# The last attention step of a diffusion-transformer layer: output projection in two banks, h in halves, top-k candidates filled in place

## Chip, cores and metric

The kernel runs on one core of a Trainium2 chip. The metric is the device time of one execution in microseconds (us). It computes everything in fp32; large products use the split of a number into a rounded part and a remainder (`hi`, `lo`), each in the fp32r format.

## What is computed

One layer over 1024 tokens of width 1024, with a context of 256 tokens. The part that matters here, cut from the reference:

```python
attn_x = latent_attention(qx, kx, vx, kc, vc)        # 12 heads of 64, 4 key heads, 1280 keys
four_x = fourier_mix(fx, w_four[l])                  # 256 columns
x = x + g1 * (jnp.concatenate([four_x, attn_x], axis=-1) @ w_out[l])
h = modulate(x, norm_ffn_g[l], sh2, sc2)             # rms_norm(x) * (1 + sc2) + sh2
# expert_choice_ffn(h, ...):
aff = jax.nn.softmax(jnp.einsum('bnd,de->bne', h, w_router), axis=-1)   # 16 experts
gates, idx = lax.top_k(aff.swapaxes(1, 2), cap)      # cap = 128 tokens of 1024 for each expert
xe = h[bidx, idx]
hid = silu(xe @ w_gate) * (xe @ w_up)                # 2048 wide
x = x + g2 * scatter_add(idx, (hid @ w_down) * gates)
return rms_norm(x, final_norm_g)
```

## The kernel before

The kernel is one program of blocks that follow each other. At the end of a block every engine waits for all others. `nc_phase_a` makes queries, keys and values. `nc_phase_b` makes the Fourier part `y_t` and then, in a block of its own, attention, output projection, normalisation and router. `nc_phase_m` picks 128 tokens for each of the 16 experts and runs the experts. On each engine the instructions of a block run in the order in which they are written; engines wait for each other by counting semaphores.

**The attention block** works on tiles of 128 tokens, `TL` = 8. A function `step(t, prev, cur)` on each engine is called for t = 0 to 8. With `cur`, it starts tile t: scores of its 12 heads; with `prev`, it finishes tile t-1. Step 8 has only `prev`. A step has 12 slots, `for i in range(NQ)`. A tile's items are 40: for each of 4 groups of three heads, 10 key tiles. For an item TensorE transposes three blocks of probabilities (L1112) into bank 4 or 5, ScalarE copies them as `pth` (L960), VectorE makes the remainder `ptl` (L1014), and two items later TensorE multiplies both with the values (L1078, L1079). The last ten items of tile t-1 (group 3) run in slots 0 to 2 of step t, with the last head's exponentials (L944) in slot 0. A group ends with a flush: at slots 0 and 3 of step t those of groups 2 and 3 of tile t-1 (sums `osum` L1022, reciprocals spread over partitions by L1122 and copied as `rbc`), and POOL writes three of the eight blocks of `mix` (L896): blocks 0 to 2 hold groups 0 and 1, blocks 3 to 5 groups 2 and 3, and blocks 6 and 7 the Fourier part, which POOL copies from `y_t` at the start of a step.

The rest of tile t-1 then goes as follows, in step t:

- Slots 4 and 5: OP0 and OP1, the two halves (512 columns) of the output projection, eight products each over the blocks of `mix` (L1132), both into PSUM bank `MB` = 7. VectorE multiplies by the gate row (L1045) and adds `x` (L1047), which gives `x2`; SP writes it to DRAM.
- Slot 6: ScalarE squares and sums `x2` (L975), POOL makes the reciprocal root (L914, L916).
- Slot 7: VectorE scales the whole of `x2` into `h2` (L1051). Slot 8: POOL adds the shift row (L901); SP writes `h2` to DRAM (L874).
- Slots 8 and 9: HT0 and HT1, four transposes of `h2` each (L1140), both into bank 7, each copied by ScalarE into `h2t` (L968, L971).
- Slot 10: RT, the router's eight products (L1145) into bank 7, maximum (L1055), exponentials. Slot 11: AF, the affinities, transposed (L1149) and copied into `aff` (L982).

All of bank 7's uses stand in one counted order: `misc_mm` counts what TensorE has written, `misc_free` what has been read, `misc(t, j)` numbers use j of step t, and `misc_free(name)` makes TensorE wait until all earlier uses were read. Banks 0 to 3 hold scores and are not used in step 8 by anything but the last exponentials of slot 0.

**The expert block.** The candidates for top-k are `cand`, 48 partitions by 512: partitions 0 to 15 hold the 16 experts' affinities of the first 512 tokens, 32 to 47 those of the other 512. POOL clears it (L1252), ScalarE fills it with two copies from `aff` (L1305, L1306), VectorE takes the highest 8 of each row sixteen times over (L1382 to L1385), then the two halves are merged and POOL gathers the first expert's tokens. SP starts with the final gain (L1241) and the expert weights (L1231).

Of the kernel before, what the change touches and what calls it, by code (L numbers as in the profile page):

```python
# [8 lines left out]
P = 128  # L9
# [24 lines left out]
UM = 256  # L34

# [51 lines left out]
def build(nc, a, out):  # L87
# [26 lines left out]
    with ctx:  # L114
        psum = ctx.enter_context(nc.psum_tensor("banks", [P, 8, 512], F32))


        ident = sb("ident", [P, P])
        ones = sb("ones", [P, P])
        G1, SH2, SC2, G2 = range(4)  # L120
        eps_c = sb("eps_c", [P, 2])
        K = ExitStack()
        ks = sb("ks", [P, NKV, KEYS], F32R, K)
        vs = sb("vs", [P, TS, NKV, 2, HD], F32R, K)
        f_tok = sb("f_tok", [P, TL, FW], F32, K)
# [4 lines left out]
        nc_phase_b(nc, ctx, sem, sb, a, K, psum, ident, ones, rows, aff, eps_c, ks, vs, f_tok, y_t,  # L130
                   q_d, mod_d, h2_d, acc_d, x_d)
        K.close()
        nc_phase_m(nc, ctx, sem, sb, a, psum, ident, rows, aff, eps_c, h2_d, acc_d, out_d, unit_in)
# [528 lines left out]
def nc_phase_b(nc, ctx, sem, sb, a, K, psum, ident, ones, rows, aff, eps_c, ks, vs, f_tok, y_t,  # L662
# [18 lines left out]
    with nc.Block() as block:  # L681
# [100 lines left out]
        "dve_order", "op_sum", "rows_in", "bias_done", "scale_done", "rows_done")}  # L782
# [8 lines left out]
    MISC0 = 2  # L791

# [44 lines left out]
    with nc.Block() as block:  # L837
        @block.sync
        def _(sp):
# [22 lines left out]
            def step(t, prev, cur):  # L862
                if cur and prev:
                    queries(t)
                if prev:
# [7 lines left out]
                    sp.wait_ge(s["h2b"], t)  # L873
# [6 lines left out]
        def _(pool):  # L880
            def step(t, prev, cur):
# [6 lines left out]
                for i in range(NQ):  # L888
# [23 lines left out]
                    if prev and i == 6:  # L912
# [3 lines left out]
                        pool.tensor_tensor(st2[:, 2:3], st2[:, 1:2], eps_c[:, 0:1], ALU.pow).then_inc(s["rstd_done"], 1)  # L916
            pool.wait_ge(s["rows_in"], 16 * 6)
# [9 lines left out]
        def _(act):  # L927
            def step(t, prev, cur):
                use = use_numbers(prev, cur)
                fl = flushes(prev, cur)  # L930
                for i in range(NQ):
# [33 lines left out]
                    if prev and i == 8:  # L965
                        act.wait_ge(s["misc_mm"], misc(t, use["HT0"]) + 1)
                        after(act, s["neg_done"], t - 1)
                        act.activation(h2t[:, 0:4, :].rearrange("p k n -> p (k n)"), psum[:, MB, :], ACT.Copy).then_inc(s["misc_free"], 1)  # L968
                    if prev and i == 9:
                        act.wait_ge(s["misc_mm"], misc(t, use["HT1"]) + 1)  # L970
                        act.activation(h2t[:, 4:8, :].rearrange("p k n -> p (k n)"), psum[:, MB, :], ACT.Copy).then_inc(s["misc_free"], 1)  # L971
# [14 lines left out]
        def _(dve):  # L986
            def step(t, prev, cur):
# [11 lines left out]
                for i in range(NQ):  # L999
# [35 lines left out]
                    if prev and i in (4, 5):  # L1035
# [29 lines left out]
        def _(pe):  # L1065
            def step(t, prev, cur):
# [15 lines left out]
                def misc_free(name):  # L1082
                    after(pe, s["misc_free"], misc(t, use[name]))

                for i in range(NQ):
# [38 lines left out]
                    if prev and i in (4, 5):  # L1124
# [5 lines left out]
                        misc_free(f"OP{j}")  # L1130
                        for k in range(KD):
                            ins = pe.matmul(psum[:, MB, :], mix[:, k, :], wout[:, k, j * 512:(j + 1) * 512],  # L1132
                                            start=(k == 0), stop=(k == KD - 1))
                        ins.then_inc(s["misc_mm"], 1)
                    if prev and i in (8, 9):
                        j = i - 8
                        pe.wait_ge(s["h2b"], t)
                        misc_free(f"HT{j}")
                        for k in range(4):
                            ins = pe.transpose(psum[:, MB, k * P:(k + 1) * P], h2[:, (4 * j + k) * P:(4 * j + k + 1) * P], ident[:, :])  # L1140
# [13 lines left out]
def nc_phase_m(nc, ctx, sem, sb, a, psum, ident, rows, aff, eps_c, h2_d, acc_d, out_d, unit_in):  # L1154
# [12 lines left out]
    H2 = 32  # L1167
    EH = H2 + E
    NH2 = N // 2
    cand = sb("cand", [EH, NH2], F32, M)  # L1170
# [26 lines left out]
        "top_order", "cand_zero", "cand_done", "merged", "carried", "top_done", "top_t", "cols_done", "idx_g", "x_in", "x_mm", "x_a", "x_b",  # L1197
# [24 lines left out]
    with nc.Block() as block:  # L1222
# [28 lines left out]
        def _(pool):  # L1251
            pool.memset(cand[:, :], 0.0).then_inc(s["cand_zero"], 1)  # L1252
# [125 lines left out]
        def _(dve):  # L1378
            dve.wait_ge(s["cand_done"], 2)
# [197 lines left out]
```

## Time and profile before

| | us |
|---|---|
| median of three runs | 2086.47 (2085.27 to 2088.32) |
| the profiled execution | 2086.9 |
| its span, first to last instruction | 2085.1 |
| TensorE matmul busy | 1858.8 (89%) |
| VectorE busy | 1606.0 (77%) |
| ScalarE busy | 1303.9 (63%) |
| POOL busy | 270.8 (13%) |
| mean granted TensorE clock | 0.954 of full |

Phase A ends near 261 us, the attention block runs from 291 to 908, the expert block from there to the end. A granted clock of 1.00 is 2.4 GHz, one of 0.50 is 1.2 GHz; a stretch in between has parts at both. Engines: PE is TensorE, PEld its weight load, DVE VectorE, ACT ScalarE, POOL GpSimd, SP SyncE, which issues most transfers. Start times are us from the start of the span.

### The profile page before, as it was taken

To read this page: it belongs to the slowest core of one execution; us is meant where nothing else is said; L and a number is where in the kernel's file an instruction comes from. 1 tells how busy PE (TensorE), PEld (TensorE's weight loads), DVE (VectorE), ACT (ScalarE), POOL (GpSimd) and SP (SyncE) were. 2 spreads that over 40 slices of the span, in tenths; PEclk is the share of its full clock that TensorE was granted. 3 is DMA by queue.
4 is the path that set the end of the run, shared out by engine and by line. 5 is a ranking of instruction groups with operands and counts; after the bars stand their busy time and mean duration, and the time that the engine had idled before them with its cause. 6 is when DMAs were issued, how large, how long until landed. Compare 5 with 4: busy or idle time off the path is not lost.

```text
span 2085.1 us, 28008 instructions
## 1 busy us (share of the span) xinstructions
PE 1858.8 (89%) x8691; PEld 1459.7 (70%) x8691; DVE 1606.0 (77%) x2065; ACT 1303.9 (63%) x1919; POOL 270.8 (13%) x291
## 2 busy tenths in 40 slices
PE   6799578998899899826999999999999999999993
PEld 3677456666666666515888888888888888888882
DVE  5577627668676766557999988889899989998983
ACT  3554127657566666524777777777777777777772
POOL 0233203101111110100111000110011001100011
PEclk8999779999999999957999999999999999999997
DMA  8356354101201110026999999999999999999985
GB/s 344 101 172 182 91 173 116 44 29 51 60 19 42 60 43 28 21 111 266 412 390 385 373 401 383 387 376 380 401 388 376 371 402 391 377 376 400 372 323 201
DMA packets 103794, 511.75 MB, mean 245 GB/s; under 512 B 12048, under 2 KB 36024, under 8 KB 53056
## 3 DMA queue, kind: packets, MB, share of 16 engines
q1 hardware_dynamic: 95824, 484.65, 61.4%
q0 software_dynamic: 4608, 16.78, 3.2%
q10 hardware_dynamic: 3312, 9.70, 1.3%
q8 instruction: 26, 0.43, 0.1%
q14 instruction: 24, 0.20, 0.0%
HBM read 481.19 MB, written 27.28 MB: 244 GB/s over the span
## 4 chain that ended last, share of the span: by engine, by line
PE 51%; issue 2%; DVE 2%; DMA 1%; ACT 0%; POOL 0%; ACTq 0%; POOLq 0%; SPq 0%
PE banks L1513 33%; PE banks L1538 16%; PE banks L1525 1%; PE banks L1494 1%; DVE topi L1384 1%; DVE top L1382 1%; DVE cand L1385 1%; DMA xe<-h_scratch,icol 0%; DMA acc_scratch<-ysc,idx_s 0%; DVE raw L1477 0%; ACT raw L1371 0%; DMA raw<-acc_scratch 0%; POOL fst L1298 0%; POOL fst L1300 0%; POOL gate_s L1281 0%
## 5 line engine op out<-in xcount | busy, mean ns | idle before, releaser
L1416 DVE TENSOR_TENSOR w_lo<-raw,w_hi 128x2048 fp32r<-128x2048 f32 x256 | 574.6, 2285 | 67.4 <-ACT w_hi L1320 67.4
L1320 ACT ACTIVATE w_hi<-raw 128x2048 fp32r<-128x2048 f32 x256 | 470.2, 1916 | 8.3 <-DMA raw<-in_w_exp 8.2
L1513 PE MATMUL banks<-w_hi,x_hi 128*128 128x512 f32 x1024 | 405.5, 396 | 1.4 <-DVE x_lo L1410 1.4
L1513 PE MATMUL banks<-w_hi,x_lo 128*128 128x512 f32 x1024 | 399.9, 390 | 0.0
L1513 PE MATMUL banks<-w_lo,x_hi 128*128 128x512 f32 x1024 | 399.4, 390 | 0.0
L1424 DVE TENSOR_TENSOR d_lo<-raw,d_hi 128x1024 fp32r<-128x1024 f32 x256 | 296.1, 1216 | 1.5 <-ACT d_hi L1342 1.4
L1342 ACT ACTIVATE d_hi<-raw 128x1024 fp32r<-128x1024 f32 x256 | 258.0, 1060 | 40.1 <-DMA raw<-in_w_exp 26.7
L1513 PEld LDWEIGHTS banks<-w_hi,x_lo 128*128 128x128 f32 x1024 | 192.7, 188 | 40.8
L1513 PEld LDWEIGHTS banks<-w_hi,x_hi 128*128 128x128 f32 x1024 | 192.9, 188 | 39.7 <-DVE x_lo L1410 1.8
L1513 PEld LDWEIGHTS banks<-w_lo,x_hi 128*128 128x128 f32 x1024 | 193.1, 189 | 38.1
L1014 DVE TENSOR_TENSOR ptl<-banks,pth 128x384 fp32r<-128x384 f32 x320 | 176.3, 554 | 56.0 <-ACT pth L960 51.7
L960 ACT ACTIVATE pth<-banks 128x384 fp32r<-128x384 f32 x320 | 157.1, 491 | 76.2 <-PE banks L1112 68.4
L944 ACT ACTIVATE pr<-banks,nb 128x512 f32<-128x512 f32 (+1 forms) x288 | 177.2, 615 | 30.9 <-DVE nb L1010 29.5
L1326 ACT ACTIVATE sil<-banks 128x512 f32<-128x512 f32 x64 | 38.3, 598 | 251.1 <-PE banks L1513 251.1
L1005 DVE TENSOR_REDUCE mx<-banks 128x1 f32<-128x512 f32 (+1 forms) x288 | 170.4, 593 | 28.9 <-PE banks L1097 28.4
L1112 PE MATMUL banks<-ident,pr 128*128 128x128 f32 x960 | 164.0, 281 | 8.2 <-DVE ptl L1014 5.0
L1096 PE MATMUL banks<-ks,qt 128*128 128x512 f32 (+1 forms) x288 | 132.5, 460 | 35.2 <-ACT pr L944 28.5
L1538 PE MATMUL banks<-d_hi,h_hi 128*128 128x512 f32 x512 | 157.9, 390 | 2.6 <-DVE h_lo L1430 2.6
L1538 PE MATMUL banks<-d_lo,h_hi 128*128 128x512 f32 x512 | 157.6, 389 | 0.0
L1538 PE MATMUL banks<-d_hi,h_lo 128*128 128x512 f32 x512 | 157.6, 389 | 0.0
L1112 PEld LDWEIGHTS banks<-ident,pr 128*128 128x128 f32 x960 | 117.4, 143 | 50.1 <-DVE ptl L1014 20.7
L1261 POOL TENSOR_TENSOR carry<-carry 128x1 f32<-128x1 f32 x31 | 19.7, 636 | 966.9 <-DVE ysc L1444 583.5
(202 smaller groups left out, 2756.8 us busy)
## 6 DMA issues: line engine op xcount, KB each, us to landing
raw<-in_w_exp SPq DMA_DIRECT2D x384, 1024.0 KB, 7.8
a_ring<-in_w_mod SPq DMA_DIRECT2D x32, 512.0 KB, 4.7
qt<-q_scratch SPq DMA_DIRECT2D x64, 192.0 KB, 3.5
a_slot<-in_w_mod SPq DMA_DIRECT2D x8, 1024.0 KB, 12.3
a_w_raw<-in_w_in SPq DMA_DIRECT2D x3, 2048.0 KB, 30.8
q_scratch<-a_qst SPq DMA_DIRECT2D x16, 384.0 KB, 3.8
a_xt<-in_x ACTq DMA_DIRECT2D x8, 512.0 KB, 3.3
xr<-in_x SPq DMA_DIRECT2D x8, 512.0 KB, 4.1
```

Source lines behind the costliest of these rows:

```text
L944: act.activation(pr[(h // 3 % 2) * 3 + h % 3][:, lo:hi], psum[:, (NCH * h + c) % 4, 0:hi - lo], ACT.Exp, bias=nb[:, h:h + 1], scale=SCALE, ...
L960: act.activation(pth[:, k % 4, :], psum[:, PTB + k % 2, 0:REP * P], ACT.Copy).then_inc(s["hi_done"], 1)
L1005: ins = dve.tensor_reduce(mx[:, i, c:c + 1], psum[:, (NCH * i + c) % 4, 0:hi - lo], AX, ALU.max)
L1014: dve.tensor_tensor(ptl[:, k % 4, :], psum[:, PTB + k % 2, 0:REP * P], pth[:, k % 4, :].bitcast(F32), ALU.subtract).then_inc(s["lo_done"], 1)
L1096: pe.matmul(o, qt[:, i, 0, :], ks[:, i // 3, lo:hi], start=True, stop=False)
L1112: ins = pe.transpose(psum[:, PTB + k % 2, r * P:(r + 1) * P], pr[(g % 2) * 3 + r][:, kt * P:(kt + 1) * P], ident[:, :])
L1320: act.activation(w_hi[which][c][:, :], raw[which][c][:, :], ACT.Copy).then_inc(s["hi_done"], 1)
L1342: act.activation(d_hi[k][:, :], raw[2][k // 2][:, k % 2 * D:(k % 2 + 1) * D], ACT.Copy).then_inc(s["d_hi_done"], 1)
L1416: dve.tensor_tensor(w_lo[which][c][:, :], raw[which][c][:, :], w_hi[which][c][:, :].bitcast(F32), ALU.subtract).then_inc(s["lo_done"], 1)
L1424: dve.tensor_tensor(d_lo[k][:, :], raw[2][k // 2][:, k % 2 * D:(k % 2 + 1) * D], d_hi[k][:, :].bitcast(F32), ALU.subtract).then_inc(s["d_l ...
L1513: i = pe.matmul(psum[:, 2 * (j % 2) + which, :], x_[par][:, k, :], w_, start=(k == 0 and w_ is hi and x_ is x_hi), stop=(k == KD - 1 and x ...
L1538: i = pe.matmul(psum[:, Y + h, :], x_[:, k, :], w_[k][:, h * 512:(h + 1) * 512], start=(j == 0 and k == 0 and x_ is h_hi and w_ is d_hi), ...
```

## The change

In step 8 alone (`not cur`), and around it:

- OP0 and OP1 get banks 0 and 1, HT0 and HT1 banks 2 and 3 (`bank_of`). RT and AF stay in bank 7.
- Ten of the sixteen products of the projection, five each over the `mix` blocks 0, 1, 2, 6 and 7 (`EARLY`), stand at the end of slots 0 and 1. Slots 4 and 5 keep blocks 3 to 5 (`LATE`).
- `h2` is made in two halves, scale and shift both on VectorE; the transposes wait for their half.
- The router's first four products wait for the first copy of `h2t`, the others for the second.
- `cand` lives on the right side of SBUF from the start of the attention block. POOL clears it there once; in step 8, slot 4, ScalarE copies what is known (all but the last tile's 128 tokens), and the last affinity copy goes into `cand` directly. The expert block starts with VectorE's first maximum.

```diff
+    EARLY, LATE = (0, 1, 2, 6, 7), (3, 4, 5)
+
+    def bank_of(name, cur):
+
+        return MB if cur else {"OP0": 0, "OP1": 1, "HT0": 2, "HT1": 3}[name]
...
-                    sp.wait_ge(s["h2b"], t)
+                    sp.wait_ge(s["h2b"], t if cur else t + 1)
...
-                    if prev and i == 8:
+                    if prev and cur and i == 8:
                         pool.wait_ge(s["h2a"], t)
                         pool.tensor_tensor(h2[:, :], h2[:, :], rows[:, SH2, :], ALU.add).then_inc(s["h2b"], 1)
...
+            pool.memset(cand[:, :], 0.0).then_inc(s["cand_zero"], 1)
             pool.wait_ge(s["rows_in"], 16 * 6)
...
-                        act.activation(h2t[:, 0:4, :].rearrange("p k n -> p (k n)"), psum[:, MB, :], ACT.Copy).then_inc(s["misc_free"], 1)
+                        act.activation(h2t[:, 0:4, :].rearrange("p k n -> p (k n)"), psum[:, bank_of("HT0", cur), :], ACT.Copy).then_inc(s["misc_free"], 1)
...
+                    if not cur and i == 4:
+
+                        act.wait_ge(s["cand_zero"], 1)
+                        act.wait_ge(s["misc_free"], misc(t, 0))
+                        act.activation(cand[0:E, :], aff[:, 0:HALF], ACT.Copy).then_inc(s["cand_done"], 1)
+                        act.activation(cand[H2:EH, 0:HALF - P], aff[:, HALF:N - P], ACT.Copy).then_inc(s["cand_done"], 1)
...
-                        act.activation(aff[:, bass.ds((t - 1) * P, P)], psum[0:E, MB, 0:P], ACT.Copy).then_inc(s["misc_free"], 1)
+                        if cur:
+                            act.activation(aff[:, bass.ds((t - 1) * P, P)], psum[0:E, MB, 0:P], ACT.Copy).then_inc(s["misc_free"], 1)
+                        else:
+                            act.activation(cand[H2:EH, HALF - P:HALF], psum[0:E, MB, 0:P], ACT.Copy).then_inc(s["misc_free"], 1)
...
-                        dve.tensor_tensor(x2[:, c], psum[:, MB, :], rows[:, G1, c], ALU.mult).then_inc(s["misc_free"], 1)
+                        dve.tensor_tensor(x2[:, c], psum[:, bank_of(f"OP{j}", cur), :], rows[:, G1, c], ALU.mult).then_inc(s["misc_free"], 1)
...
+                        if not cur:
+                            for c in (slice(0, 512), slice(512, D)):
+                                chain(dve.scalar_tensor_tensor(out=h2[:, c], in0=x2[:, c], scalar=st2[:, 2:3], in1=rows[:, SC2, c],
+                                                               op0=ALU.mult, op1=ALU.mult))
+                                dve.tensor_tensor(h2[:, c], h2[:, c], rows[:, SH2, c], ALU.add).then_inc(s["h2b"], 1)
+                            continue
...
+                def out_part(j, ks_, first, last):
+                    for k in ks_:
+                        ins = pe.matmul(psum[:, bank_of(f"OP{j}", cur), :], mix[:, k, :], wout[:, k, j * 512:(j + 1) * 512],
+                                        start=(first and k == ks_[0]), stop=(last and k == ks_[-1]))
+                    return ins
...
-                        misc_free(f"OP{j}")
-                        for k in range(KD):
-                            ins = pe.matmul(psum[:, MB, :], mix[:, k, :], wout[:, k, j * 512:(j + 1) * 512],
-                                            start=(k == 0), stop=(k == KD - 1))
-                        ins.then_inc(s["misc_mm"], 1)
+                        if cur:
+                            misc_free(f"OP{j}")
+                            out_part(j, range(KD), True, True).then_inc(s["misc_mm"], 1)
+                        else:
+                            out_part(j, LATE, False, True).then_inc(s["misc_mm"], 1)
+                    if not cur and i in (0, 1):
+                        pe.wait_ge(s["exp_done"], NS * TL)
+                        pe.wait_ge(s["mix_done"], 4 * t - 2)
+                        pe.wait_ge(s["ymix_done"], t)
+                        out_part(i, EARLY, True, False)
...
-                        pe.wait_ge(s["h2b"], t)
-                        misc_free(f"HT{j}")
+                        pe.wait_ge(s["h2b"], t if cur else t + j)
+                        if cur:
+                            misc_free(f"HT{j}")
...
-                        misc_free("RT")
+                        misc_free("RT" if cur else "HT1")
                         for k in range(KD):
+                            if not cur and k == KD // 2:
+                                misc_free("RT")
                             ins = pe.matmul(psum[:, MB, 0:E], h2t[:, k, :], wrt[:, k, :], start=(k == 0), stop=(k == KD - 1))
...
-            pool.memset(cand[:, :], 0.0).then_inc(s["cand_zero"], 1)
             pool.wait_ge(s["cols_done"], 2)
...
-            act.wait_ge(s["cand_zero"], 1)
-            act.activation(cand[0:E, :], aff[:, 0:NH2], ACT.Copy).then_inc(s["cand_done"], 1)
-            act.activation(cand[H2:EH, :], aff[:, NH2:N], ACT.Copy).then_inc(s["cand_done"], 1)
...
-            dve.wait_ge(s["cand_done"], 2)
```

## Rows read from the trace of the kernel before

**Rows 1.** Page, part 4: the chain that ended last, shares by engine.
```profile
PE 51%; issue 2%; DVE 2%; DMA 1%; ACT 0%; POOL 0%; ACTq 0%; POOLq 0%; SPq 0%
```

**Rows 2.** Stretches: length, busy us (count) by engine, granted clock, DMA share, GB/s.
```profile
872.00:908.00 36.00, 23.22 (x61) 12.22 (x61) 5.34 (x10) 3.68 (x8) 4.07 (x4) 0.78 0.07 29
...
1000.00:1050.00 50.00, 50.00 (x230) 41.46 (x229) 45.91 (x33) 36.61 (x32) 8.68 (x5) 1.00 1.00 403
```

**Rows 3.** Timeline, last step, the items' rhythm: start, us, engine, line, operation, [idle before].
```profile
865.70 0.33 PE L1079 MATMUL banks<-ptl,vs 128*128 128x384 f32 x1
...
866.06 0.52 PE L1112 MATMUL banks<-ident,pr 128*128 128x128 f32 x3
...
867.75 0.55 PE L1112 MATMUL banks<-ident,pr 128*128 128x128 f32 x3
```

**Rows 4.** Timeline, last step, the output projection until x2 is done and squared.
```profile
874.99 8.76 PE L1132 MATMUL banks<-wout,mix 128*128 128x512 f32 x16 [1.71 <-POOL mix L896]
...
884.63 7.10 PE L1132 MATMUL banks<-wout,mix 128*128 128x512 f32 x16 [0.88 <-DVE x L1045]
885.14 0.19 PEld L1132 LDWEIGHTS banks<-wout,mix 128*128 128x128 f32 x1 [0.24 <-issue]
885.57 0.19 PEld L1132 LDWEIGHTS banks<-wout,mix 128*128 128x128 f32 x1 [0.24 <-issue]
...
892.50 0.69 DVE L1047 TENSOR_TENSOR x<-x,xr 128x512 f32<-128x512 f32 x1
...
893.22 1.06 ACT L975 ACTIVATE junk<-x 128x1024 f32<-128x1024 f32 x1 [19.42 <-DVE x L1047]
```

**Rows 5.** Stretches around the projection and the router: columns as in rows 2.
```profile
862.00:864.00 2.00, 2.00 (x9) 1.53 (x8) 1.01 (x2) 1.21 (x5) 0.42 (x1) 0.50 0.00 0
864.00:866.00 2.00, 1.67 (x8) 0.90 (x7) 1.11 (x2) 1.60 (x7) 0.58 (x1) 0.84 0.00 0
866.00:872.00 6.00, 5.68 (x33) 3.78 (x32) 4.14 (x9) 3.16 (x7) 0.83 (x1) 1.00 0.01 3
874.00:880.00 6.00, 5.01 (x8) 2.28 (x9) 0.00 (x0) 0.00 (x0) 0.94 (x1) 0.72 0.00 0
896.00:908.00 12.00, 6.09 (x25) 5.00 (x25) 1.38 (x5) 1.56 (x4) 2.34 (x1) 0.50 0.11 44
```

**Rows 6.** Timeline, last step, h2 and the router's product.
```profile
895.37 1.28 DVE L1051 SCALAR_TENSOR_TENSOR h<-x,st,rows 128x1024 f32<-128x1024 f32 x1 [2.18 <-POOL st L916]
896.74 2.34 POOL L901 TENSOR_TENSOR h<-h,rows 128x1024 f32<-128x1024 f32 x1 [1.40 <-DVE h L1051]
899.10 0.34 SPq L874 DMA_DIRECT2D h_scratch<-h  x1
...
899.13 1.11 PE L1140 MATMUL banks<-ident,h 128*128 128x128 f32 x4 [7.39 <-POOL h L901]
...
902.15 0.60 ACT L971 ACTIVATE h2t<-banks 128x512 f32<-128x512 f32 x1 [1.27 <-PE banks L1140]
...
902.80 3.59 PE L1145 MATMUL banks<-wrt,h2t 128*128 128x16 f32 x16 [0.69 <-ACT h2t L971]
906.43 0.17 DVE L1055 TENSOR_REDUCE lg<-banks 128x1 f32<-128x16 f32 x1 [9.77 <-PE banks L1145]
```

**Rows 7.** Timeline, the last affinity copy, the block's end and the first maximum.
```profile
908.13 0.27 ACT L982 ACTIVATE aff<-banks 16x128 f32<-16x128 f32 x1 [0.94 <-PE banks L1149]
908.66 0.52 POOL L1252 MEMSET cand<- 48x512 f32 x1 [9.59 <-POOLq L837]
909.01 0.35 SPq L1241 DMA_DIRECT2D fgain<-in_final_norm_g  x1
...
909.86 0.63 ACT L1306 ACTIVATE cand<-aff 16x512 f32<-16x512 f32 x1
910.52 0.69 DVE L1382 MAX8 top<-cand 48x8 f32<-48x512 f32 x1 [2.87 <-ACT cand L1306]
```

**Rows 8.** DMA issues from 840 to 960 us: KB each, median us to landing.
```profile
h_scratch<-h SPq DMA_DIRECT2D x2, 512.0 KB, 2.7
```

More of the change, by code:

```diff
@@ L34 @@
 UM = 256
+H2 = 32
+EH = H2 + E
 SCALE = HD ** -0.5 * HD
@@ L129, in build @@
         aff = ctx.enter_context(nc.sbuf_tensor("aff", [E, N], F32, side="right"))
-        nc_phase_b(nc, ctx, sem, sb, a, K, psum, ident, ones, rows, aff, eps_c, ks, vs, f_tok, y_t,
+        cand = ctx.enter_context(nc.sbuf_tensor("cand", [EH, N // 2], F32, side="right"))
+        nc_phase_b(nc, ctx, sem, sb, a, K, psum, ident, ones, rows, aff, cand, eps_c, ks, vs, f_tok, y_t,
                    q_d, mod_d, h2_d, acc_d, x_d)
         K.close()
-        nc_phase_m(nc, ctx, sem, sb, a, psum, ident, rows, aff, eps_c, h2_d, acc_d, out_d, unit_in)
+        nc_phase_m(nc, ctx, sem, sb, a, psum, ident, rows, cand, eps_c, h2_d, acc_d, out_d, unit_in)
 def after(eng, sem_, v):
@@ L659, in nc_phase_a, with nc_phase_b @@
     return unit_in
-def nc_phase_b(nc, ctx, sem, sb, a, K, psum, ident, ones, rows, aff, eps_c, ks, vs, f_tok, y_t,
+def nc_phase_b(nc, ctx, sem, sb, a, K, psum, ident, ones, rows, aff, cand, eps_c, ks, vs, f_tok, y_t,
                q_d, mod_d, h2_d, acc_d, x_d):
@@ L781, in nc_phase_b @@
         "x2_done", "ss_done", "rstd_done", "mean", "h2a", "h2b", "h2_out", "x2_out", "neg_done", "lexp",
-        "dve_order", "op_sum", "rows_in", "bias_done", "scale_done", "rows_done")}
+        "dve_order", "op_sum", "rows_in", "bias_done", "scale_done", "rows_done", "cand_zero", "cand_done")}
     q_in = [sem(f"b_q_in{g}") for g in range(NKV)]
@@ L967, in step @@
                         after(act, s["neg_done"], t - 1)
[L968 removed]
+                        act.activation(h2t[:, 0:4, :].rearrange("p k n -> p (k n)"), psum[:, bank_of("HT0", cur), :], ACT.Copy).then_inc(s["misc_free"], 1)
                     if prev and i == 9:
                         act.wait_ge(s["misc_mm"], misc(t, use["HT1"]) + 1)
[L971 removed]
+                        act.activation(h2t[:, 4:8, :].rearrange("p k n -> p (k n)"), psum[:, bank_of("HT1", cur), :], ACT.Copy).then_inc(s["misc_free"], 1)
+                    if not cur and i == 4:
[3 more added lines that the diff above has]
+                        act.activation(cand[H2:EH, 0:HALF - P], aff[:, HALF:N - P], ACT.Copy).then_inc(s["cand_done"], 1)
                     if prev and i == 6:
@@ L1129, in step @@
                         pe.wait_ge(s["ymix_done"], t)
-                        misc_free(f"OP{j}")
-                        for k in range(KD):
-                            ins = pe.matmul(psum[:, MB, :], mix[:, k, :], wout[:, k, j * 512:(j + 1) * 512],
-                                            start=(k == 0), stop=(k == KD - 1))
-                        ins.then_inc(s["misc_mm"], 1)
+                        if cur:
[8 more added lines that the diff above has]
+                        out_part(i, EARLY, True, False)
                     if prev and i in (8, 9):
                         j = i - 8
-                        pe.wait_ge(s["h2b"], t)
-                        misc_free(f"HT{j}")
+                        pe.wait_ge(s["h2b"], t if cur else t + j)
+                        if cur:
+                            misc_free(f"HT{j}")
                         for k in range(4):
-                            ins = pe.transpose(psum[:, MB, k * P:(k + 1) * P], h2[:, (4 * j + k) * P:(4 * j + k + 1) * P], ident[:, :])
+                            ins = pe.transpose(psum[:, bank_of(f"HT{j}", cur), k * P:(k + 1) * P], h2[:, (4 * j + k) * P:(4 * j + k + 1) * P], ident[:, :])
                         ins.then_inc(s["misc_mm"], 1)
                     if prev and i == 10:
-                        misc_free("RT")
+                        misc_free("RT" if cur else "HT1")
                         for k in range(KD):
+                            if not cur and k == KD // 2:
+                                misc_free("RT")
                             ins = pe.matmul(psum[:, MB, 0:E], h2t[:, k, :], wrt[:, k, :], start=(k == 0), stop=(k == KD - 1))
@@ L1151, in nc_phase_b, with nc_phase_m @@
     B.close()
-def nc_phase_m(nc, ctx, sem, sb, a, psum, ident, rows, aff, eps_c, h2_d, acc_d, out_d, unit_in):
+def nc_phase_m(nc, ctx, sem, sb, a, psum, ident, rows, cand, eps_c, h2_d, acc_d, out_d, unit_in):
     G1, SH2, SC2, G2 = range(4)
@@ L1165, in nc_phase_m @@
     raw = [[sb(f"raw{w}{c}", [P, CH], F32, M) for c in range(2)] for w in range(3)]
-    H2 = 32
-    EH = H2 + E
     NH2 = N // 2
-    cand = sb("cand", [EH, NH2], F32, M)
     top = sb("top", [EH, CAP], F32, M)
@@ L1196, in nc_phase_m @@
     s = {n: sem("m_" + n) for n in (
-        "top_order", "cand_zero", "cand_done", "merged", "carried", "top_done", "top_t", "cols_done", "idx_g", "x_in", "x_mm", "x_a", "x_b",
+        "top_order", "merged", "carried", "top_done", "top_t", "cols_done", "idx_g", "x_in", "x_mm", "x_a", "x_b",
         "gate_mm", "up_mm", "sil_done", "hid_done", "ht_mm", "ht_done", "down_mm", "y_done", "y_out", "sel_done",
```

## The prediction

> **What bounds the kernel now.** I read the views from coarse to fine. The page's chain of work that ended last [rows 1] is mostly TensorE, on two lines of the expert phase. The stretches [rows 2] say why: from 1000 us on TensorE is busy all the time at the full granted clock, while in the 36 us from 872 to 908, the end of the attention phase, it is busy for 23.2 us of 36, no other engine for more than 5.4 us, and the clock is at 0.78. So that stretch is a serial chain, one engine at a time, and the expert phase starts when it is over: its weight loads, its top-k and its gather all stand behind the end of the attention block. Nothing there runs by an absolute time, so I count every microsecond taken from the chain between 866 and 910.5 us as one microsecond of the kernel. The timeline of that stretch, with the granted clock beside it, is what the sum is made of [rows 3 to 7].
>
> All of the change sits in the last step of the attention phase (no queries of its own, only the leftovers of tile 7) and in the first instructions of the expert phase. Steps 0 to 7 keep their instructions, but for a memset of `cand` on POOL at the start, which lies ahead of POOL's wait for the loads of `rows`: nothing.
>
> **Part 1: output projection.** Before, both halves use one PSUM bank. OP0 takes 8.76 us, then VectorE must read the bank (TensorE idles 0.88 us), OP1 takes 7.10 us, and VectorE needs two operations more, 1.46 us with their hand-overs, from 884.63 + 7.10 = 891.73 to 892.50 + 0.69 = 893.19, where `x2` is done [rows 4]. From 874.99 that is 18.20 us.
>
> A product here is two matmul records of 0.43 us each (885.14 to 885.57 in [rows 4]), 0.86 us at the full clock. OP0 has 8 products and so 6.9 us of work plus about 0.2 of latency, but took 8.76, since part of it ran at 1.2 GHz [rows 5]: the stretch from 874 to 880 has a mean of 0.72, and with two levels, 1.00 and 0.50, that is 0.28 x 6 / 0.5 = 3.4 us at the lower one, in which 1.7 us of work is left undone.
>
> After: ten of the sixteen products (the rows of `mix` of groups 0, 1 and the Fourier part) move ahead, five behind slot 0 and five behind slot 1. They are not removed. What they wait for is there: the last exponentials lie inside slot 0 and the two `mix` groups are a step old. At slot 0's end (about 866.0) the clock is back at 1.00 [rows 5], so they add 10 x 0.86 = 8.6 us to TensorE's queue. Does TensorE have room there? Hardly: between one item's last matmul and the next transpose it idles (866.06 - 865.70 - 0.33 =) about 0.03 us by the modelled ends, perhaps 0.2 us really; ScalarE and VectorE drain at most their two buffers in each pause and then stand idle. Items k and k+2 are 1.69 us apart (866.06 to 867.75 in [rows 3]), a loop over three engines that starts again after each pause with the same length. So the insertion costs 8.6 us, at most 0.4 us less; I take 8.6.
>
> Behind the last `mix`, six products are left. TensorE idled 1.71 us before OP0 [rows 4], and that bubble stays as it is, since it belongs to the last group's sums. I take the clock to fall again as it did [rows 5]: 6 x 0.86 + 1.7 + 0.2 = 7.06 us for both halves, the second in a bank of its own, so without the 0.88 us wait, and VectorE's work on OP0 lies beside OP1's three products (1.46 against 2.6 us). Then 1.46 us for OP1 on VectorE: 8.52 us. Sum: 18.20 - 8.52 - 8.58 = **1.1 us saved**. Nearly all of the move itself is exchange; the gain is the wait and that VectorE's part is no longer in between. Bounds: 0.9 (a little extra latency at each of two more accumulation groups) to 1.5 with the fall; 2.8 to 3.2 if the clock doesn't fall there.
>
> [...]
>
> **Part 2: h and the router.** From the start of `h2` (895.37) to the first use of the router's result (906.43) are 11.06 us [rows 6]: VectorE 1.28 over 1024 columns, POOL 2.34, TensorE's four transposes 1.1, ScalarE's copy 0.60, again both, since the halves share a bank, then 3.59 us for the 16 router records. All this at a clock of 0.50 [rows 5] (the idle time of TensorE before it, 7.39 us by the bracket, gets shorter but stays several us).
>
> After: VectorE does both operations in halves. The half of the first is not in the trace; 512 columns of a two-operand VectorE operation cost 0.69 [rows 4], 1024 columns of this one 1.28, so it lies between 0.64 and 0.74, I take 0.70. First half ready: 0.70 + 0.04 + 0.69 + 0.04 = 1.47 instead of 3.76. Second half 1.47 later, at 2.94. TensorE: transposes 1.47 to 2.6, then it waits for the second half, 2.94 to 4.05. ScalarE copies the first bank (2.6 to 3.2) under that, and the second, 4.1 to 4.7. The router's first eight records need only the first copy: 4.05 to 5.85, which covers the second copy; the other eight, 5.85 to 7.65. Router's result read at 7.68 instead of 11.06: **3.4 us saved**, bounds 3.1 (0.05 more at each of six hand-overs) to 3.6.
>
> What the halves cost: the Trainium skill ("VectorE: DVE Perf Modes", section "The TRN2 errata") says that each VectorE instruction on SBUF pays a fixed time whatever its size, and advises large tiles. By it whole rows on VectorE, about 1.28 + 1.22, would bring the last column at 2.6 instead of 2.94, but the first column too; TensorE would then do both halves from 2.6 and be at about 4.9 instead of 4.05. The rows (1.28 for 1024 against 0.69 for 512) bear the fixed part out; the halves still win by the overlap.
>
> `h2` goes to DRAM after both halves, as before after one addition. That write was issued at 899.10 and takes 2.7 us to land [rows 6, 8], the block's end was at 908.5; the distance shrinks from 9.4 to some 6.8 us and still covers it.
>
> **Part 3: top-k candidates.** Before, the last affinity copy ends at 908.13 + 0.27 = 908.40; behind the block's end POOL clears `cand` (908.66), ScalarE copies twice (0.63 each), and VectorE's first maximum starts at 910.52 [rows 7]. After, two copies (the second shorter) stand in ScalarE's queue at slot 4, about 1.2 us within the 19.42 us in which it waited for `x2` (at 893.22 in [rows 4]); without that cover they would cost 1.2. The clear is a step at the start. The last copy goes straight into `cand`. VectorE then starts when the block lets it: POOL's first instruction came 0.26 behind the last copy, SP's first 0.61 behind it [rows 7]. I take 0.30: 908.70. **1.8 us saved**, bounds 1.5 to 1.9.
>
> **Sum.** 1.1 + 3.4 + 1.8 = 6.3 us. The profiled execution took 2086.9 us around a span of 2085.1; 2086.9 - 6.3 = 2080.6. The median of the runs shown is 2086.47, 0.4 lower, within their scatter of 3 us. I predict **2080.5 us**.
>
> **Rivals.**
> - *The clock does not fall at the late products.* For it: ten dense products lie a few us earlier and the bubble may meet the throttle otherwise; against it: the bubble is unchanged, and a fall came there. It gives 6.3 + 1.7 = 8.0 us saved, 2086.9 - 8.0 = 2078.9 us. Chance 0.27.
> - *The early products find less or more: part of them at 1.2 GHz.* The clock was at 0.50 from 862 to 864, at 0.84 on the mean of the next 2 us and at 1.00 after 866 [rows 5]; if that earlier fall comes some us later, up to two products are slow, 1.7 us lost, and the fall at the end comes as well: 4.6 us saved, 2082.3. Chance 0.10.
> - *The gain is taken back in the expert phase*, by a gather or weight load that does not start earlier in step. For it: VectorE and DMA are nearly full there. Against: all start behind the same block end [rows 7], and TensorE is busy throughout [rows 2]. It would take half of the sum, about 3 us: 2083.7. Chance 0.05.
> - *Slower:* all ten early products at half clock, because after the pauses TensorE's load looks too thin: 10 x 0.86 = 8.6 us more, against 6.3 saved, so 2.3 us slower, 2089.2. It decides from about eight products at half speed. Against: the loop around them ran at 1.00 and they are the densest work of all. Chance 0.02 (a smaller one of the same sort lies in the case before).
> - Main case, near the sum: 0.56.
>
> **How the numbers follow.** About 0.2% (4.2 us) is what a measurement of this kernel can tell from no change, so faster means below about 2082.3. Main case and first rival lie there, the second on the edge, the third above. Faster 0.86, same 0.12, slower 0.02. The range goes from the first rival with its bounds and the scatter (2078.3) to the edge of the second (2082.6).
>
> **What would show it.** In the profile after: two blocks of ten matmul records each (`wout`) near 866 and 872, at 0.43 us a record; the last `mix` near 883.5; twelve records behind it without a gap in the middle, and a granted clock of 0.5 there or not; `h2` with two pairs of 0.7 us on VectorE and none on POOL; 7.7 us from `h2`'s start to the router's reduction; 0.3 us from the last copy to the first maximum, which then starts near 904.2 instead of 910.52; the expert phase unchanged in length. It is wrong if the early blocks take over 5 us each, if the item loop gets slower behind them, if VectorE's first maximum comes over 0.7 us behind the last copy, or if the expert phase is longer.

## The result

| | before | changed |
|---|---|---|
| first comparison, 5 executions each: median, us | 2086.47 (2085.22 to 2088.32) | 2077.33 (2073.13 to 2082.94) |
| ratio, 95% interval | | 0.9950 (0.9935 to 0.9965) |
| all executions of this study: count, mean, median, us | 100, 2087.4, 2087.6 (2082.5 to 2092.4) | 34, 2080.7, 2080.6 (2073.1 to 2090.6) |
| profiled execution: time, span, us | 2086.9, 2085.1 | 2073.1, 2071.3 |

The kernel is faster by some 0.3%: small, but the interval lies clear of 1 (the quotient of the two medians alone is 0.9956). The first median, 2077.33, lies 1.0 us under the predicted range of 2078.3 to 2082.6. Three more comparisons gave 0.9955 (0.9942 to 0.9968), 0.9974 (0.9962 to 0.9985) and 0.9979 (0.9967 to 0.9991); the last two share their executions of before. Over all executions the gain is 6.6 us (2087.38 - 2080.74), with a 95% interval of about 5.3 to 7.9, worked out from standard deviations of 2.5 and 3.6 us for one execution.

**The profile after**, last step, timeline: the early products, the late ones, `x2` and the copies of candidates.

```profile
861.65 4.45 PE L1111 MATMUL banks<-wout,mix 128*128 128x512 f32 x10
...
865.94 0.49 PE L1142 MATMUL banks<-ident,pr 128*128 128x128 f32 x3
...
867.61 0.55 PE L1142 MATMUL banks<-ident,pr 128*128 128x128 f32 x3
...
868.35 4.45 PE L1111 MATMUL banks<-wout,mix 128*128 128x512 f32 x10
...
872.64 0.49 PE L1142 MATMUL banks<-ident,pr 128*128 128x128 f32 x3
...
877.71 0.61 ACT L985 ACTIVATE cand<-aff 16x512 f32<-16x512 f32 x1
877.96 0.99 POOL L904 TENSOR_TENSOR mix<-osum,rbc 64x384 f32<-64x384 f32 x1 [14.03 <-ACT rbc L973]
878.35 0.52 ACT L986 ACTIVATE cand<-aff 16x384 f32<-16x384 f32 x1
...
879.00 5.42 PE L1111 MATMUL banks<-wout,mix 128*128 128x512 f32 x12 [1.71 <-POOL mix L904]
...
881.88 0.69 DVE L1063 TENSOR_TENSOR x<-banks,rows 128x512 f32<-128x512 f32 x1 [4.12 <-PE banks L1111]
...
885.91 1.06 ACT L990 ACTIVATE junk<-x 128x1024 f32<-128x1024 f32 x1 [7.04 <-DVE x L1065]
```

Each early block holds TensorE for 4.29 us (861.65 to 865.94, 868.35 to 872.64), ten records of 0.43. The two halves' late products run as one, 5.42 us, and VectorE works on the first half (from 881.88) beside them. The idle 1.71 us ahead is as it was [rows 4]. From 879.00 to the squaring are 6.9 us, against 18.2 before.

Stretches of the profile after, columns as in [rows 2]. The clock is at 1.00 on the late products and at 0.50 on transposes and router:

```profile
876.00:879.00 3.00, 1.26 (x4) 0.65 (x4) 0.56 (x1) 2.00 (x4) 0.99 (x1) 1.00 0.01 3
879.00:884.00 5.00, 5.00 (x12) 2.20 (x12) 1.38 (x2) 0.00 (x0) 0.00 (x0) 1.00 0.00 0
884.00:888.00 4.00, 0.42 (x1) 0.00 (x0) 1.38 (x2) 1.15 (x2) 0.72 (x2) 0.95 0.32 130
888.00:898.00 10.00, 5.84 (x25) 5.05 (x25) 3.89 (x9) 1.82 (x5) 0.02 (x1) 0.50 0.13 53
```

Timeline after, `h2`, the router and the first maximum, to be laid beside [rows 6, 7]:

```profile
888.06 0.75 DVE L1071 SCALAR_TENSOR_TENSOR h<-x,st,rows 128x512 f32<-128x512 f32 x1 [2.18 <-POOL st L924]
888.84 0.69 DVE L1073 TENSOR_TENSOR h<-h,rows 128x512 f32<-128x512 f32 x1
889.45 0.74 DVE L1071 SCALAR_TENSOR_TENSOR h<-x,st,rows 128x512 f32<-128x512 f32 x1
889.59 1.12 PE L1176 MATMUL banks<-ident,h 128*128 128x128 f32 x4 [5.17 <-DVE h L1073]
890.23 0.69 DVE L1073 TENSOR_TENSOR h<-h,rows 128x512 f32<-128x512 f32 x1
...
890.98 1.12 PE L1176 MATMUL banks<-ident,h 128*128 128x128 f32 x4 [0.27 <-DVE h L1073]
891.88 3.44 PE L1183 MATMUL banks<-wrt,h2t 128*128 128x16 f32 x16
892.13 0.60 ACT L980 ACTIVATE h2t<-banks 128x512 f32<-128x512 f32 x1 [0.79 <-PE banks L1176]
...
895.36 0.17 DVE L1079 TENSOR_REDUCE lg<-banks 128x1 f32<-128x16 f32 x1 [4.44 <-PE banks L1183]
...
897.06 0.27 ACT L1000 ACTIVATE cand<-banks 16x128 f32<-16x128 f32 x1 [0.94 <-PE banks L1187]
897.63 0.69 DVE L1411 MAX8 top<-cand 48x8 f32<-48x512 f32 x1 [1.04 <-PEq L845]
```

From the start of `h2` to the reduction are 7.30 us (11.06 before). The router starts 0.25 us ahead of ScalarE's second copy and isn't held up by it. From the last copy's end (897.33) to the maximum are 0.30 us (2.12 before).

**Where the profiled 13.8 us went.** Between the two profiled executions, POOL's first `mix` write of the last step comes 4.2 us earlier after the change (859.37 against 863.58), in code that is the same in both. From there to the first maximum are 38.26 against 46.94 us, 8.7 less. From that to the end are 1173.67 against 1174.58, 0.9 less. So 5.1 of 13.8 us lie outside all that was changed. Is that the change, or the draw?

### The profile page after: what moved, and what is told of

It reads as the page before. It is cut to its first block, busy times and chain, and to the rows that moved or that the text cites. A ratio compares the mean times of both kernels' runs of the same rounds, so it can differ in the third digit from the quotient of the medians.

```text
span 2071.3 us, 28011 instructions
## 1 busy us (share of the span) xinstructions
PE 1853.0 (89%) x8691; PEld 1456.3 (70%) x8691; DVE 1608.0 (78%) x2068; ACT 1303.4 (63%) x1919; POOL 282.9 (14%) x290
## 4 chain that ended last, share of the span: by engine, by line
PE 51%; issue 2%; DVE 2%; DMA 1%; ACT 0%; POOL 0%; ACTq 0%; POOLq 0%; SPq 0%
PE banks L1542 33%; PE banks L1567 16%; PE banks L1554 1%; PE banks L1523 1%; DVE topi L1413 1%; DVE top L1411 1%; DVE cand L1414 1%; DMA xe<-h_scratch,icol 0%; DMA acc_scratch<-ysc,idx_s 0%; DVE raw L1506 0%; ACT raw L1401 0%; DMA raw<-acc_scratch 0%; POOL fst L1332 0%; POOL fst L1334 0%; POOL gate_s L1315 0%
## 5 line engine op out<-in xcount | busy, mean ns | idle before, releaser
L1295 POOL TENSOR_TENSOR carry<-carry 128x1 f32<-128x1 f32 x31 | 43.5, 1404 | 952.5 <-DVE ysc L1473 583.4
```

## The experiments

All times of stretches below run from that first `mix` write of the last step (in slot 0) to the squaring of `x2`, from `h2`'s start to the router's reduction, from the last affinity copy's end to the first maximum, and in all from the first `mix` write to the first maximum.

The "fall" below is one of the granted clock, from 2.4 to 1.2 GHz.

| kernel | executions | mean us | ratio (95%) | mix to squaring | h2 to reduction | copy to maximum | in all | maximum to end |
|---|---|---|---|---|---|---|---|---|
| before, profile 1 | | | | 29.64 (fall) | 11.06 | 2.12 | 46.94 | 1174.58 |
| e9_before_again | 12 | 2086.5 | 0.9997 (0.9986 to 1.0009) | 29.70 (fall) | 11.06 | 2.12 | 46.99 | 1175.88 |
| changed, profile 1 | 5 | 2077.7 | 0.9950 (0.9935 to 0.9965) | 26.54 | 7.30 | 0.30 | 38.26 | 1173.67 |
| e1_repeat | 5 | 2080.3 | 0.9955 (0.9942 to 0.9968) | 26.54 | 7.30 | 0.31 | 38.27 | 1176.11 |
| e10_after_again | 12 | 2080.6 | 0.9974 (0.9962 to 0.9985) | 27.89 (fall) | 7.31 | 0.30 | 39.61 | 1173.67 |
| e11_after_third | 12 | 2082.4 | 0.9979 (0.9967 to 0.9991) | 26.60 | 7.30 | 0.30 | 38.32 | 1173.69 |
| e2_part1 | 12 | 2085.4 | 0.9987 (0.9977 to 0.9997) | 27.88 (fall) | 11.06 | 2.13 | 45.19 | 1174.11 |
| e3_part2 | 11 | 2083.9 | 0.9980 (0.9971 to 0.9989) | 27.68 | 7.30 | 2.13 | 41.23 | 1176.14 |
| e4_part3 | 12 | 2086.0 | 0.9988 (0.9977 to 0.9998) | 27.68 | 11.05 | 0.30 | 43.15 | 1173.71 |
| e5_no_early | 6 | 2081.4 | 0.9964 (0.9952 to 0.9977) | 26.56 | 7.30 | 0.30 | 38.29 | 1174.25 |
| e6_fill_projection | 5 | 2079.4 | 0.9957 (0.9944 to 0.9970) | 26.21 | 5.36 | 0.30 | 35.99 | 1174.32 |
| e7_fill_gather | 5 | 2074.8 | 0.9941 (0.9928 to 0.9954) | 26.53 | 5.37 | 0.30 | 36.32 | 1171.10 |
| e12_fill_again | 6 | 2076.6 | 0.9946 (0.9929 to 0.9964) | 26.21 | 6.32 | 0.30 | 36.94 | 1171.48 |
| e8_whole_rows | 9 | 2082.3 | 0.9971 (0.9957 to 0.9985) | 27.88 (fall) | 8.03 | 0.31 | 40.34 | 1175.94 |

Behind the executions the columns are of one profile each. "fall" marks a profile in which the granted clock was at 1.2 GHz for a part of the products behind the last `mix` write.

### e1, e9, e10, e11: both kernels again, unaltered

> The changed kernel once more, unaltered. Between the end of slot 0 of the last step and the first maximum the profile after took 35.98 us against 44.49 before: 8.5 us of the 13.8 us between the two spans. 4.4 us more lay ahead of slot 0's end, in code that the change does not touch. Theory A (those 4.4 us are scatter from execution to execution): the first product of the output projection in slot 0 starts here somewhere between 861 and 867 us, the chain of 36 us repeats to 0.2 us if the clock does not fall at the late products and is 1.7 us longer if it does, and the median is 2077 to 2080. Theory B (the change makes the phases ahead faster, by placement in memory or in the instruction stream): slot 0 ends at 861.7 again within 1 us, and the median is within 1 us of 2077.

> The kernel before, once more, for its spread and one more profile. Theory A (where the clock falls is drawn anew in each execution): from the first mix write of the last step to the first maximum 44.9 to 45.3 us if the clock stays up at the projection, 46.6 to 47.0 if it falls; the phases ahead of it end anywhere within 10 us; median within 1.5 us of 2088. Theory B (the profile of before shows its rule, 46.94 with the fall each time): 46.9 again.

> The changed kernel, once more, for its spread and one more profile. Theory A: from the first mix write to the first maximum 37.9 to 38.3 us if the clock stays up at the late products, 39.6 to 40.0 if it falls. Like for like that is 7.0 us under before, so the mean over many executions lies 6.5 to 8 us under that of before. Theory B (there is a gain outside the chain as well, 1.7 us by the ten runs so far): the mean stays 8.5 us or more under it.

> The changed kernel a fourth time, same as the one before: five more times for the mean, and one more draw of where the clock falls.

Theory A holds in the main. In e1 the same kernel has its first `mix` write at 868.82, 9.5 us later than in the profile after, which rules out placement as the reason why the profile after was early there (e1 expected it somewhat less late: it put the first product of slot 0 between 861 and 867, and it came behind 868.82). e9 by itself can't tell its two theories apart, since the fall came again (46.99 us); that the same projection also runs without one is shown by e3 and e4 below. e11's 38.32 lies 0.02 above its range. The phase that makes keys and values ends at different times too. Timelines, VectorE's first instruction behind it, in the profile after:

```profile
258.89 2.36 DVE L694 TENSOR_TENSOR pm<-f_tok 128x1024 f32<-128x1024 f32 x2 [7.89 <-PEq L211]
```

and in e4, which has the same code there:

```profile
266.15 2.36 DVE L694 TENSOR_TENSOR pm<-f_tok 128x1024 f32<-128x1024 f32 x2 [7.89 <-PEq L211]
```

The clock is a part of it: its mean over the first 80 us is 0.87 in the profile after and 0.83 in e4. It isn't all of it, for the profile before has 0.83 as well and gets there at 261.00.

```profile
0.00:80.00 80.00, 50.31 (x221) 31.93 (x222) 43.26 (x82) 37.35 (x60) 7.74 (x25) 0.87 0.61 245
```

```profile
0.00:80.00 80.00, 49.63 (x212) 31.96 (x213) 43.27 (x82) 36.26 (x57) 6.98 (x25) 0.83 0.60 240
```

Over whole executions the two go together more closely. In the 34 of the changed kernel, time and mean granted clock have a correlation of -0.89: three at 0.957 took 2076.3 us on average, three at 0.952 took 2085.8.

Whether the clock falls at the late products differs between profiles of one kernel as well. Stretch and timeline of e10, the changed kernel with a fall there:

```profile
882.00:884.00 2.00, 2.00 (x3) 0.97 (x4) 0.00 (x0) 0.00 (x0) 0.00 (x0) 0.54 0.00 0
884.00:886.00 2.00, 2.00 (x4) 0.73 (x4) 0.00 (x0) 0.00 (x0) 0.00 (x0) 0.60 0.00 0
```

```profile
882.00 7.11 PE L1111 MATMUL banks<-wout,mix 128*128 128x512 f32 x12 [1.71 <-POOL mix L904]
```

7.11 against 5.42 us: the fall costs 1.69. The code ahead and the 1.71 us of idle time are the same in both. It isn't a draw of its own, though: in all eleven profiles without idle work it goes with the clock in slot 0. With early products, the clock was still down in slot 0 in three profiles (after, e1, e11), with no fall behind, and up in three (e10, e2, e8), all with the fall. Without early products it is the other way round: before and e9 had both, e3, e4 and e5 neither. Why is not shown.

Like for like, and with the same clock in slot 0, the stretch is 11.02 + 16.66 before (e4) and 19.25 + 6.96 after (e6, whose idle work lies off this path): 27.68 against 26.21. No profile without idle work has early products and neither of the two falls, so a single pair of profiles can show anything for part 1 from 0.2 us lost (27.68 to 27.88) to 3.1 saved (29.64 to 26.54). If each pattern comes half the time, which is not shown, the mean is again some 1.5.

The mean of the changed kernel's later 29 executions is 2081.3, 6.1 under before. The gain of 8.5 us or more of theory B does not repeat; e10 alone, at 6.4 us under its comparison's before, and e11 at 4.6 lie just under and well under theory A's 6.5 to 8. Over all 34 it is 6.6 us, and the stretches like for like give 1.47 + 3.76 + 1.82 = 7.05.

### e2, e3, e4: one part alone

```diff
e2   OP in banks 0 and 1, ten products early; HT in bank 7, h2, router, candidates as before
e3   h2 in halves, HT in banks 2 and 3, router by halves; OP in bank 7, candidates as before
e4   candidates filled in place; the rest as before
```

> Only the output projection in two banks with ten products early; h2, transposes, router and candidates as before. Theory A: from slot 0's end to x2 done, 27.1 us before, 24.2 here if the clock stays up at the late products (2.9 saved), 25.9 if it falls (1.2 saved); time 1 to 3 us under the kernel before. Theory B (gain outside the chain): more than 4 us under it. Rival of the prediction, the clock at half in the early products: each block of ten records takes up to 8.6 us instead of 4.3.

> Only h2 in halves on VectorE, transposes in two banks, router by halves; the output projection in bank 7 and the candidates as before. Theory A: 7.3 us from the start of h2 to the router's reduction instead of 11.06, so 3.8 us saved, time 3 to 4.5 under the kernel before. Of the prediction's own numbers, 7.7 us and 3.4 saved. Theory B: more than 6 us under it. If the halves cost an instruction's fixed time that matters, it would be under 3 us.

> Only the candidates filled in place; all else as before. Theory A: 0.30 us from the last affinity copy to the first maximum instead of 2.11, 1.8 us saved, time 1 to 2.6 under the kernel before. Theory B, the variant of it in which the placement of cand in SBUF or the clear at the block's start matters for the phases ahead: more than 4 us under it, with slot 0's end several us earlier than 866.

The means lie 2.4, 3.9 and 1.8 us under 2087.8, before's mean in that comparison. Their intervals are some 2 us to either side, so they bear the parts out, but don't size them; the stretches do: part 1 27.88 against 29.64 and 29.70 with a fall in both (1.8, of which 0.33 is slot 0, see below), part 2 3.76, part 3 1.82, and none of them has an effect on the others' stretch. In e4 there is no fall at the projection, though its code there is that of before: TensorE's sixteen records of OP0 take 7.13 us instead of 8.76 [rows 4], behind the same idle time.

```profile
884.32 7.13 PE L1105 MATMUL banks<-wout,mix 128*128 128x512 f32 x16 [1.72 <-POOL mix L904]
```

Early products at half clock, the rival on the slower side, did not come: from the first `mix` write to the end of the last one are 19.23 to 19.65 us in all nine profiles with early products, so no block was slow in any. The two values within that range are the clock in slot 0. Where it is still at 1.2 GHz there, as in [rows 5] at 862, the stretch is 0.33 longer, with early products (19.58 against 19.25) and without (11.36 against 11.02). Such a fall ahead of the early products came in four of the nine; it never reached into them.

### e5: no product early

```diff
                         else:
-                            out_part(j, LATE, False, True).then_inc(s["misc_mm"], 1)
-                    if not cur and i in (0, 1):
-                        pe.wait_ge(s["exp_done"], NS * TL)
-                        pe.wait_ge(s["mix_done"], 4 * t - 2)
-                        pe.wait_ge(s["ymix_done"], t)
-                        out_part(i, EARLY, True, False)
+                            out_part(j, range(KD), True, True).then_inc(s["misc_mm"], 1)
```

> The changed kernel with all sixteen products of the projection in slots 4 and 5 (two banks kept, none early). Theory A (the move of ten products is an exchange, only the two banks and the clock count): from the first mix write of the last step to the squaring of x2 26.5 to 26.9 us if the clock stays up, 1.7 more if it falls, against 26.54 with the early products and the clock up; time within 1.5 us of the changed kernel. Rival (the early products fill idle TensorE time): 2 to 8 us more here.

Timeline of e5, all sixteen products behind the last `mix` write:

```profile
880.03 14.00 PE L1111 MATMUL banks<-wout,mix 128*128 128x512 f32 x32 [1.72 <-POOL mix L904]
```

14.00 us of products behind the flush, 8.58 more than the late ones alone, while the stretch ahead is 11.02 instead of 19.25. In all 26.56 us against 26.21 with the same clock in slot 0: the move of ten products is worth 0.35 us, two banks the other 1.1. The exchange of theory A is shown, on one profile each.

### e6, e7, e12: idle work against the clock's fall

Products that nobody reads, into banks that nobody uses then. The first stand in slot 4 ahead of the wait for `mix`, the second behind the late products; the third, behind the top-k transposes, are in e7 and e12 only:

```diff
+                        if not cur and j == 0:
+                            fill((512, 256))
...
+                            if j == 1:
+                                fill((512,) * 5)
...
+            for _ in range(7):
+                pe.matmul(psum[:, Y, :], ident[:, :], rows[:, G2, 0:512], start=True, stop=True)
```

> The changed kernel with idle work for TensorE, whose result nobody reads: products of 512 and 256 columns ahead of the late products (1.3 us, idle there 1.7) and five of 512 behind them (4.3 us, idle there 5.2). Theory A (what the late products, the transposes and the router take is set by the granted clock, and that by the idle time ahead): the late products stay at 5.4 us, each four transposes fall from 1.12 to about 0.7 and the router from 3.44 to about 1.8; from the start of h2 to the router's reduction 5.4 to 5.8 us instead of 7.30, time 1.5 to 3 us under the changed kernel. Rival (the latency of these small products sets them, not the clock): 7.3 us, and the time is the same or longer by what the idle work delays.

> As the one before, and seven products of 512 columns behind the top-k transposes, in the 9.4 us in which TensorE waits for the first gather. Theory A: at full clock the eight transposes take about 1.3 us less the overlap instead of 2.0, and the first products of the experts 0.23 us apiece from the start instead of 0.43 for the first ten, 2 to 2.5 us less from the first maximum to the end; time 4 to 5 us under the changed kernel. Rival: VectorE or the weight loads bound the first expert, and the gain is gone within it.

> The kernel with idle work before and behind the late products and behind the top-k transposes, once more, since five executions of it say little beside a spread of some 3.5 us. By its first profile the stretch from the first mix write to the first maximum is 36.0 to 36.4 us (1.9 under the changed kernel with the clock up at the late products) and from the first maximum to the end 1171.1 (2.6 to 5 under it); so its mean should lie 4.5 to 6 us under the changed kernel's 2080.7 and 11 to 13 under before. Rival: the length behind the first maximum is only the draw of the first profile, 1174 again, and 2 us remain.

Timeline of e6, from the second set of idle products to the reduction:

```profile
891.15 4.46 PE L1111 MATMUL banks<-wout,ident 128*128 128x512 f32 x10
...
896.48 0.66 PE L1184 MATMUL banks<-ident,h 128*128 128x128 f32 x4 [0.88 <-DVE h L1073]
...
897.87 0.66 PE L1184 MATMUL banks<-ident,h 128*128 128x128 f32 x4 [0.73 <-DVE h L1073]
...
898.36 1.92 PE L1191 MATMUL banks<-wrt,h2t 128*128 128x16 f32 x16
```

The same instructions take 0.66 instead of 1.12 and 1.92 instead of 3.44 us: the granted clock was 1.00 on the transposes and 0.94 on the mean of the router, against 0.50 before. It had set their times. 1.94 us of the chain are gone. In e12 the clock fell within the router (2.86 us), and 1 us was left of that gain. At the late products there was no fall in three profiles; without idle work there was one in five of eleven, so three profiles show little on that.

Timeline of e7 at the gather:

```profile
931.93 8.05 PE L1523 MATMUL banks<-rows,ident 128*128 128x512 f32 x14
941.41 1.10 PE L1533 MATMUL banks<-ident,xe 128*128 128x128 f32 x8 [1.42 <-DMA xe<-h_scratch,icol]
```

and the same transposes in the profile after, in 1.97 us:

```profile
942.71 1.97 PE L1523 MATMUL banks<-ident,xe 128*128 128x128 f32 x8 [9.28 <-DMA xe<-h_scratch,icol]
```

From the first maximum to the end e7 and e12 take 1171.10 and 1171.48 us, all others 1173.67 to 1176.14. Some 2 us of it are there at the eleventh record of the first expert's products, which starts 50.28 us behind the first maximum in e7 and 52.21 in the profile after. Over eleven executions the mean is 2075.8 us, 5.0 under the changed kernel and 11.6 under before. This version beats both; its ratio to before is 0.9941 (0.9928 to 0.9954) and 0.9946 (0.9929 to 0.9964). The expectations missed in sizes: e6's mean is 1.3 us under the changed kernel (1.5 to 3 expected), e7's 5.9 (4 to 5), e12's 4.2 (4.5 to 6), and e12's stretch is 36.94 us, not 36.0 to 36.4, by the fall in the router.

### e8: h2 in whole rows on VectorE

```diff
-                            for c in (slice(0, 512), slice(512, D)):
+                            for c in (slice(0, D),):
```

> The changed kernel with h2 made on VectorE in whole rows of 1024 (two operations instead of four), transposes in two banks and router by halves as changed. Worked out: 1.28 + 0.04 + about 1.22 + 0.04 = 2.6 us to the first transpose, 1.8 for both sets, then 3.44 for the router: 7.8 to 8.2 us from the start of h2 to the router's reduction against 7.30 with halves; time 0.5 to 1 us over the changed kernel. Rival (an instruction's fixed time is what halving costs, by the Trainium skill, page VectorE: DVE Perf Modes, section on the errata): 7.3 or less.

8.03 us against 7.30: the halves are worth 0.73. The mean is 1.6 us over the changed kernel, above the 0.5 to 1 expected, with a standard deviation of some 1.5 us for that difference; and the fall at the late products, which its profile has, is no part of the edit. VectorE's two instructions took 1.28 and 1.23 there, four in halves 0.75, 0.69, 0.74 and 0.69. The fixed part of which the Trainium skill ("VectorE: DVE Perf Modes", section "The TRN2 errata") speaks is there, 2.87 us of VectorE's time against 2.51, and the overlap wins.

## Why the prediction was right and where it was wrong

- **What bounds the kernel, and that the chain's gain reaches the end**: right. 7.05 us less in the chain, 6.6 us (5.3 to 7.9) in the mean of 34 against 100 executions. The rival in which the expert phase takes half back is out: from the first maximum to the end the kernels without idle work there take 1173.7 to 1176.1 us with no order between them.
- **Part 1**, predicted 1.1 with the same clock before and after: 1.47 with the clock up in both, 1.8 - 0.33 with a fall in both. The insertion costs 19.25 - 11.02 = 8.23, not 8.6; the "at most 0.4 us less" was the value. e5 bears out that the gain is the wait for the bank and VectorE's work beside the products, as said (1.1 of 1.47 us).
- **Part 2**, predicted 3.4 (bounds 3.1 to 3.6): 3.76, outside the bounds. The step that failed is "second transposes 2.94 to 4.05, then the router": TensorE took the router's first product 0.90 us behind the start of the transposes (891.88 - 890.98), not 1.1. The 1.1 of [rows 6] is the time to the last result, and the next instruction on the same engine need not wait for it. So the router started 3.82 us behind `h2`'s start instead of 4.05, and from there to the reduction were 3.48 instead of 3.63. VectorE's half of 0.75 instead of 0.70 cost nothing at the end, since the second transposes started at 2.92 (2.94 forecast).
- **Part 3**, predicted 1.8 with 0.30 us to the first maximum: 1.82 with 0.30.
- **The clock at the late products**: the main case took it "to fall again as it did", and the first rival its absence (2078.9). The profile after had no fall there (5.42 us), so its stretch up to the first maximum was 8.7 us shorter than before's, not 6.3. Both occur with either code: the same projection without a fall is in e3 and e4, the changed one with it in e10. It was wrong to let one profile decide it; that puts 1.7 us into the term that another profile of the same kernel doesn't have. The rival's reason, that the bubble may meet the throttle otherwise behind the early products, fits the pattern above: with the clock down in slot 0, as in the profile before, there was no fall in three of three.
- **The number.** The first median is 2077.33, 1.0 under the range. The step of the prediction that failed is "within their scatter of 3 us": three executions of before within 3 us were taken for the kernel's spread, and the range ends at 2078.3, 0.6 below the 2078.9 of its own rival, for bounds and scatter together. The hundred executions of before cover 10 us, the 34 of the changed kernel 17 (2073.1 to 2090.6, median 2080.6). By random draws from these (an estimate), a median of five has a standard deviation of some 1.9 us and a median of three of before, where the sum starts, 1.8: some 2.6 together, beside the bounds of the terms. Of the distance to 2080.5, 0.75 is mis-sized terms (7.05 - 6.3). Why the rest fell on the first comparison stays open: five drawn from the 34, these five among them, have a median of 2077.4 or less in about 1 of 100 draws. What the record shows is that their mean granted clock was higher (0.956 against 0.954 in the later 29), in line with the shorter times. What made it so, no run tells.
- **Luck.** The forecast of 2080.5 is within 0.2 us of the mean of the 34. The sum was 0.75 too small, and it started from a profile and a median 0.5 to 0.9 us under before's mean of 2087.4; the two errors nearly cancel.

## What to carry to other kernels

Work moved ahead on the engine that bounds the stretch is an exchange; count what it frees (a bank, a wait, another engine's turn), not what it moves. For an instruction with another behind it on the same engine, take the distance of starts, not the duration. Before sizing a change of a few microseconds, look for the terms that differ between executions of one kernel, such as a clock that falls at an idle spot: compare stretches like for like, and give a median of few executions the spread of many.

## What the runs showed of the hardware

- The end of the unchanged phases varies by 14 us between profiles of kernels that are the same there (first `mix` write of the last step from 859.4 to 873.2), and, over whole executions of the changed kernel, time and mean granted clock have a correlation of -0.89.
- 1.71 us of idle TensorE behind a busy stretch was followed by a fall of the clock in some executions and not in others, at the same place of the same code (5.42 or 7.11 us for the late products). In the eleven profiles it went with whether the clock had been down in slot 0, one way with the early products and the other way without.
- Idle products in a gap of 5.2 us kept the clock at 2.4 GHz and brought four fp32 transposes from 1.12 to 0.66 us and sixteen records of the router from 3.44 to 1.92.
